# Encoder layer on one core: ssm_b loads moved into SyncE's queue, and another order of the last group's residual, norm and stores

## The chip, the cores and the metric

One Trainium2 chip, one core of it. The metric is the device time of one execution in microseconds; the kernel before took 2082.99 us, the median of three runs (2081.72 to 2086.61). The core has five engines that run their own instruction streams and meet by semaphores: TensorE (PE), VectorE (DVE), ScalarE (ACT), GpSimd (POOL) and SyncE (SP), which here only issues DMAs. GpSimd issues DMAs too, on a software queue of its own.

## The reference

A single encoder layer on 512 tokens of width 1024, all in float32:

```python
h = h + mixer_block(rms_norm(h, g_mix), ...)            # S5 state space + latent attention
h = h + memory_cross_attention(rms_norm(h, g_mem_q), rms_norm(mem, g_mem_kv), ...)
h = h + peer_ffn(rms_norm(h, g_peer), ...)
return rms_norm(h, g_final)

def rms_norm(x, g):
    return x * rsqrt(mean(x * x, -1) + 1e-6) * g
```

The state-space part takes its input matrices from `ssm_b_re` and `ssm_b_im` (2 directions x 32 groups x 64 states x 16 channels each), scaled by a factor made of the decay. `peer_ffn` finds, for each token and each of 8 heads, the best 16 of 16384 experts, gathers a row of `peer_u` and one of `peer_v` for each, and adds up 16 rows of `peer_v`, weighted by a gate times gelu of the dot product of the token with the row of `peer_u`.

## The kernel before, in words

Tokens lie on partitions in 4 tiles of 128. The kernel is written engine by engine, each block in program order; all order between engines comes from semaphores.

**Head.** SyncE issues the constants, the small state-space parameters, the four tiles of x (L582), the norm gains (L588), then weight slabs: `load_slab(n)` (L595) fills one of 3 slots of 1 MB. The first two are the two halves of the input projection ("u"), the third the first latents ("c"). Behind them come copies of `peer_u` and `peer_v` side by side into one table `uv_rows` in HBM (`copy_rows`, L590), which go on between the later slabs. GpSimd issues the four ssm_c loads (L2055) and the four ssm_b loads (L2059), all counted on the semaphore `d_ssm`, then clears some tiles.

ScalarE sums the squares of each x tile as it lands (`squares`, L683), takes the root once VectorE has added epsilon, then an exponential and a sine for the decay (L729 to L731). GpSimd waits for these (L2069) and builds powers of the decay and tables (L2070 to L2127), first small ones, then up to 128 x 1024. PE transposes the normalised x, transposes ssm_c (it waits for all eight loads, L1694), and multiplies by the u slabs. VectorE needs ssm_b from L1198 on. ScalarE takes the first output matrices of GpSimd in `windows` (L754). PE then goes on with lag products, which SyncE spreads with 8 loads per quarter (L618).

**Tail.** `peer_ffn` runs as 32 groups: g = 4 h + t, for head h and token tile t. For each of the 16 experts (slots) of a group GpSimd gathers 128 rows of 8 KB (`row`, L2130) into a ring of 12; it waits until PE has finished the slot that held the place. VectorE makes the dot product (`dot_products`, L1530), ScalarE gelu, gate and a diagonal matrix of the weights (`weigh`, L994), two slots at a time, PE multiplies the diagonal with the row's second half and adds up in PSUM (`slots`, L1951): banks 0 and 1 for even tiles, 2 and 3 for odd ones. VectorE adds the sum to the residual H after a group (`take_sum`, L1539), in the course of the next one.

In the last head each tile also gets its final norm: `final_variance` (square sum over 1024 and epsilon, VectorE, L1547), `final_root` (ScalarE, L990), `final_rows` (reciprocal and scaling by it and by g_final, VectorE, L1552), store (SyncE, L656). For tiles 0 to 2 this lies among the dots of the last group, with all three roots taken together ahead of slots 10 and 11; each is stored as soon as it is scaled. For tile 3 it comes after the last sum. ScalarE swaps its function table (ACT_TABLE_LOAD) when it goes from gelu to the root and back.

Of the kernel before, what the change touches and what calls it, by code (L numbers as in the profile page):

```python
# [232 lines left out]
def encoder_layer(nc, x, mem, positions, g_mix, w_in, b_gate, ssm_lam_re, ssm_lam_im, ssm_log_dt,  # L233
# [4 lines left out]
    with ctx:  # L238
# [3 lines left out]
        def sem(name):  # L242
            return ctx.enter_context(nc.semaphore(name))
# [25 lines left out]
        def reg(lo, *shape, base=R, parts=P):  # L269
# [93 lines left out]
        act_row = reg(27792, TOPK)  # L363
        gel = reg(27808, TOPK)
        junk = reg(17408, D)
        junk1, junk2 = reg(24064, D), held[:, :]
# [9 lines left out]

        d_cst, d_vec, d_par, d_ssm = [sem(n) for n in ("d_cst", "d_vec", "d_par", "d_ssm")]
        d_x = [sem(f"d_x{t}") for t in range(NT)]
# [30 lines left out]
            sem(n) for n in ("dots", "gate_ready", "diag_done", "v_summed")]  # L409
        acc_taken, final_done = sem("acc_taken"), sem("final_done")  # L410
        xg_done = sem("xg_done")

# [161 lines left out]
        def _(sp):  # L574
# [30 lines left out]

            for n in range(SLOTS):
                load_slab(n)
            copy_rows("first")
            for n in range(SLOTS, 5):
# [41 lines left out]
            for h in range(1, PH):  # L651
                sp.wait_ge(q_filled, h * 2)
                sp.dma_start(qw, rows(w_peer_q, h * 256, h * 256 + 256)).then_inc(qw_in, 16)
            for t in range(NT):
                sp.wait_ge(final_done, t + 1)
                sp.dma_start(out[0, P * t:P * t + P, :], xn[:, t, :]).then_inc(d_out, 16)  # L656
            sp.wait_ge(d_out, 16 * NT)

# [7 lines left out]
        def sumsq(k, t):  # L666
            return stat[:, 16 * k + t:16 * k + t + 1]
# [3 lines left out]
        def _(act):  # L671
# [49 lines left out]
            for d in range(2):  # L721
                settle(act.activation(parrow[2][:, 64 * d:64 * d + 64],
                                      dtrow[:, d:d + 1].to_broadcast([G, 64]), ACT.Copy))
            act.activation(parrow[3].rearrange("g (j c) -> g j c", j=CH),
                           drow[:, 0:CG].unsqueeze(1).to_broadcast([G, CH, CG]), ACT.Copy).then_inc(par_rows, 1)
            squares(0, xn, FT[:, 0:2, :].rearrange("p k t -> p (k t)"))

# [282 lines left out]
            def head(h, first=False, last=False):  # L1010
                for t in range(1 if first else 0, NT):
                    g = h * NT + t
                    for b in range(TOPK // 2):
# [6 lines left out]
                        if b == 7 and (not last or t < 2):  # L1020
                            gate_exponentials(g + 2)
                        if last and t == NT - 1 and b == 5:
                            for early in range(NT - 1):
                                final_root(early)
                        if last and t == NT - 1 and b == 7:
                            weigh(g, b, (14,))
                            weigh(g, b, (15,))
                        else:
                            weigh(g, b, (2 * b, 2 * b + 1))
# [25 lines left out]
            head(PH - 1, last=True)  # L1055
            settle(act.activation(gel[:, 0:1], stat[:, 68:69], ACT.Sqrt))
            final_root(NT - 1)


        @block.vector  # L1060
        def _(dve):
# [135 lines left out]
            tt(sm[:, 85, :], sm[:, 85, :], sm[:, 81, :], ALU.mult)  # L1197
            dve.wait_ge(d_ssm, 16 * 8)  # L1198
            fr, fi = (sm[:, 84 + r, :].unsqueeze(2).to_broadcast([P, G, CG]) for r in range(2))
# [358 lines left out]
            def head(h, first=False, last=False):  # L1558

                for t in range(1 if first else 0, NT):  # L1560
# [17 lines left out]
                    if ahead and (not first or t != 2):  # L1578
                        sub_keys((t + 2) % NT)
                    dot_products(g, t, range(5, 8))  # L1580
                    take_sum(g + (-1), (t - 1) % NT)
# [6 lines left out]
                    if last and t == NT - 1:  # L1588
                        final_variance(2)
                        dot_products(g, t, range(10, 11))  # L1590
                        dve.wait_ge(d_frow, 16)
                        for early in range(NT - 1):
                            dot_products(g, t, range(11 + early, 12 + early))
                            final_rows(early)
                        dot_products(g, t, range(14, TOPK))
                    elif last and t == 2:
# [50 lines left out]
            head(PH - 1, last=True)  # L1647
            take_sum(NG - 1, NT - 1)
            final_variance(NT - 1)
            final_rows(NT - 1)  # L1650


        @block.tensor
        def _(pe):
# [38 lines left out]

            pe.wait_ge(d_ssm, 16 * 8)  # L1694
            for r in range(2):
# [253 lines left out]
            early_turns(0)  # L1949
            mem_out(1, 1)  # L1950
            def slots(g, t, some):  # L1951

                for s in some:
                    i = g * TOPK + s
                    pe.wait_ge(diag_done, g * TOPK + (s + 1))
                    v = rings[i % RING]
                    for n in range(2):
                        last = pe.matmul(ps[2 * (t % 2) + n][:, :], diag[s], v[:, D + 512 * n:D + 512 * n + 512],  # L1958
                                         start=(s == 0), stop=(s == TOPK - 1))
                    last.then_inc(v_summed, 1)  # L1960
# [46 lines left out]
            def head(h, first=False, last=False):  # L2007
                for t in range(1 if first else 0, NT):
                    g = h * NT + t
                    ahead = t < 2 and not last  # L2010
                    if not first or t >= 2:
                        pe.wait_ge(acc_taken, g - 1)
                    for n in range(TOPK):
                        slots(g, t, range(n, n + 1))
# [25 lines left out]
        def _(pool):  # L2040
# [12 lines left out]
            for r, w in enumerate((ssm_c_re, ssm_c_im)):  # L2053
                for d in range(2):
                    pool.dma_start(Craw[r][:, :, 64 * d:64 * d + 64],  # L2055
                                 w[0, d].rearrange("(b g) c p -> (g c) b p", b=NB)).then_inc(d_ssm, 16)
            for r, w in enumerate((ssm_b_re, ssm_b_im)):
                for d in range(2):
                    pool.dma_start(bb[r][64 * d:64 * d + 64, :, :],  # L2059
                                 w[0, d].rearrange("g p c -> p g c")).then_inc(d_ssm, 16)  # L2060

# [112 lines left out]
```

## Time and profile before

| | us |
|---|---|
| median of 3 runs (lowest, highest) | 2082.99 (2081.72, 2086.61) |
| profiled execution, as timed | 2079.8 |
| its span in the profile | 2077.5 |
| PE busy | 1784.5 (86%) |
| VectorE busy | 1421.3 (68%) |
| ScalarE busy | 734.3 (35%) |
| GpSimd busy | 709.5 (34%) |

The span runs from the first to the last record of the profiled execution; the time of that execution is 2.3 us longer. Shares of busy time are averages over very different stages. The start and the end of the kernel are short and serial, so there the order in time is to be read, and the waits, not the shares. "DMA share" is the mean busy share of the 16 DMA engines; one engine alone is about 6 to 7%.

### The profile page before, as it was taken

Reading aid. Unit: us, or ns where it says so; the run is one execution under the profiler, and the core shown is the slowest. Engines: PE = TensorE matmul, PEld = TensorE weight load, DVE = VectorE, ACT = ScalarE, POOL = GpSimd, SP = SyncE. Lnnn points to the kernel's source line nnn. Section 1 sums busy time; section 2 is a strip of 40 time slices with the busy share of each in tenths; the row PEclk is TensorE's granted clock in tenths of the full one; section 3 lists DMA queues with packets and bytes.
Section 4 is the critical chain, followed back from the end, with each engine's and each line's share of the span. In section 5 each row is a group of like instructions: output and inputs, shape, how many; then the busy total and the mean of one; then the engine's idle time right before and its main releaser. Section 6 shows DMA issues by size and latency. Waiting matters only on the chain.

```text
span 2077.5 us, 19311 instructions
## 1 busy us (share of the span) xinstructions
PE 1784.5 (86%) x5959; PEld 994.7 (48%) x5959; DVE 1421.3 (68%) x2951; ACT 734.3 (35%) x1949; POOL 709.5 (34%) x659
## 2 busy tenths in 40 slices
PE   5998899999999999899789879888969878987876
PEld 5656434787997675334334334333423333433332
DVE  5894775434453277887777787787677777777765
ACT  3344443222333234343243333333333433343333
POOL 6990000000000034354444444344444444444441
PEclk9998899999999999999989989989999999999999
DMA  9775999888999989999999999999999999999996
GB/s 263 206 197 128 249 294 274 263 249 263 306 282 327 305 323 388 417 421 421 417 421 421 417 421 421 418 421 421 417 418 421 415 408 414 414 418 418 421 414 263
DMA packets 199313, 737.24 MB, mean 355 GB/s; under 512 B 31222, under 2 KB 97963, under 8 KB 133675
## 3 DMA queue, kind: packets, MB, share of 16 engines
q0 software_dynamic: 74112, 537.95, 62.7%
q1 hardware_dynamic: 125098, 198.07, 32.1%
q8 instruction: 47, 0.77, 0.2%
q14 instruction: 56, 0.45, 0.1%
HBM read 731.78 MB, written 136.31 MB: 418 GB/s over the span
## 4 chain that ended last, share of the span: by engine, by line
PE 44%; DMA 25%; DVE 16%; issue 7%; POOL 4%; ACT 4%; SPq 0%; DVEq 0%; ACTq 0%; POOLq 0%
PE bank L1671 23%; PE bank L1958 17%; DMA R<-uv_rows,R 10%; DMA WS<-uv_rows,R 8%; DMA slabs<-uv_rows,R 6%; PE bank L1992 3%; DVE R L1535 2%; PE bank L1660 1%; POOL WS L2049 1%; POOL R L2049 1%; DVE R L1485 1%; DVE R L1488 1%; DVE R L1486 1%; DVE R L1516 1%; DVE R L1519 1%
## 5 line engine op out<-in xcount | busy, mean ns | idle before, releaser
L1958 PE MATMUL bank<-R 128*128 128x512 f32 x1368 | 675.7, 639 | 149.1 <-ACT R L1008 149.0
L2134 POOL DMA_INDIRECT R<-uv_rows,R x342 | 384.8, 1125 | 511.2 <-PE bank L1958 486.7
L1535 DVE CUSTOM_DVE_ANT_0 R<-R,XN 128x1024 f32<-128x1024 f32 x342 | 419.5, 1227 | 169.6 <-DMA R<-uv_rows,R 155.9
L1958 PEld LDWEIGHTS bank<-R 128*128 128x128 f32 x1368 | 272.5, 204 | 525.3 <-issue 311.5
L1001 ACT ACTIVATE R<-R 128x2 f32<-128x2 f32 (+1 forms) x257 | 52.1, 203 | 803.5 <-DVE R L1535 803.1
L2134 POOL DMA_INDIRECT WS<-uv_rows,R x86 | 95.6, 1112 | 687.4 <-DVEq L1522 587.0
L1671 PE MATMUL bank<-R 128*64 128x64 f32 (+6 forms) x776 | 186.0, 387 | 20.0 <-DVE R L1232 7.4
L1958 PE MATMUL bank<-slabs,R 128*128 128x512 f32 x336 | 164.2, 630 | 29.0 <-ACT R L1008 29.0
L1958 PE MATMUL bank<-WS,R 128*128 128x512 f32 x344 | 164.1, 617 | 25.8 <-ACT R L1008 25.8
L1008 ACT ACTIVATE R<-cst,R 128x128 f32<-128x128 f32 x512 | 177.7, 394 | 8.4
L1535 DVE CUSTOM_DVE_ANT_0 R<-WS,XN 128x1024 f32<-128x1024 f32 x86 | 105.4, 1226 | 45.2 <-DMA WS<-uv_rows,R 41.6
L2134 POOL DMA_INDIRECT slabs<-uv_rows,R x84 | 96.8, 1152 | 110.1 <-PE bank L1958 102.5
L1671 PEld LDWEIGHTS bank<-R 128*64 128x64 f32 (+3 forms) x776 | 93.4, 160 | 84.5 <-issue 58.6
L1535 DVE CUSTOM_DVE_ANT_0 R<-slabs,XN 128x1024 f32<-128x1024 f32 x84 | 102.9, 1225 | 42.6 <-DMA slabs<-uv_rows,R 39.5
L1104 DVE TENSOR_TENSOR WSr<-slabs,WSr 128x1024 fp32r<-128x1024 f32 (+2 forms) x46 | 58.4, 1270 | 101.0 <-ACT WSr L709 101.0
L1003 ACT ACTIVATE R<-R 128x1 f32<-128x1 f32 x512 | 123.1, 287 | 8.5
L1992 PE MATMUL bank<-FT,slabs 128*128 128x512 f32 (+1 forms) x256 | 123.2, 574 | 2.4 <-ACT FT L681 2.4
L1958 PEld LDWEIGHTS bank<-slabs,R 128*128 128x128 f32 x336 | 67.0, 202 | 119.4 <-issue 81.3
L1958 PEld LDWEIGHTS bank<-WS,R 128*128 128x128 f32 x344 | 66.8, 197 | 114.3 <-issue 78.5
L1671 PE MATMUL bank<-Rr,WSr 128*128 128x512 f32 (+1 forms) x448 | 95.4, 366 | 0.0
L1671 PEld LDWEIGHTS bank<-Rr,WSr 128*128 128x128 f32 x448 | 77.7, 189 | 13.7
L1071 DVE TENSOR_TENSOR R<-R 128x512 f32<-128x512 f32 (+4 forms) x75 | 65.0, 867 | 18.2 <-PE bank L1671 10.7
(228 smaller groups left out, 2157.3 us busy)
## 6 DMA issues: line engine op xcount, KB each, us to landing
uv_rows<-in_peer_u SPq DMA_DIRECT2D x8, 4096.0 KB, 23.6
uv_rows<-in_peer_v SPq DMA_DIRECT2D x8, 4096.0 KB, 35.3
uv_rows<-in_peer_v SPq DMA_DIRECT2D x10, 2048.0 KB, 13.3
uv_rows<-in_peer_u SPq DMA_DIRECT2D x9, 2048.0 KB, 14.0
uv_rows<-in_peer_u SPq DMA_DIRECT2D x11, 1024.0 KB, 8.2
slabs<-in_w_in SPq DMA_DIRECT2D x17, 512.0 KB, 5.3
slabs<-in_w_mem_kv SPq DMA_DIRECT2D x8, 1024.0 KB, 11.8
slabs<-in_w_peer_q SPq DMA_DIRECT2D x8, 1024.0 KB, 25.4
```

Of the source, the lines that this page charges most:

```text
L1001: settle(act.activation(gel[:, new], act_row[:, new], ACT.Gelu_apprx_tanh))
L1003: ins = act.activation(wgt[:, s:s + 1], gel[:, s:s + 1], ACT.Copy, scale=gate[g % NT][:, s:s + 1])
L1008: act.activation(diag[s], ident, ACT.Copy, scale=wgt[:, s:s + 1]).then_inc(diag_done, 1)
L1071: step(dve.tensor_tensor(out, a, b, op))
L1104: dve.tensor_tensor(lo, src, hi, ALU.subtract).then_inc(w_lo, 1)
L1485: lstep(dve.max_index(ix[:, 0:8], v[:, 0:8], vals))
L1535: dve.tensor_tensor_reduce(prod, rings[i % RING][:, 0:D], xn[:, t, :], 1.0, 0.0, ALU.mult, ALU.add, act_row[:, s:s + 1]).then_inc(dots, 1)
L1671: last = pe.matmul(dst, lhs, rhs, start=(n == 0), stop=(n == len(terms) - 1))
L1958: last = pe.matmul(ps[2 * (t % 2) + n][:, :], diag[s], v[:, D + 512 * n:D + 512 * n + 512], start=(s == 0), stop=(s == TOPK - 1))
L1992: ins = pe.matmul(ps[4 + s][:, cols], qw[:, k, columns(s)], FT[:, k, cols], start=(k == 0), stop=(k == KD - 1))
L2049: step(pool.tensor_tensor(out, a, b, op))
L2134: pool.indirect_dma_start(out=rings[i % RING], out_offset=None, in_=UV, in_offset=bass.IndirectOffsetOnAxis(ap=idx[t][:, s:s + 1], axis=0) ...
```

## The change

Head: the four ssm_b loads leave GpSimd's queue and are issued by SyncE after the first two slabs, ahead of the third; they get a semaphore of their own, `d_ssb`. ScalarE takes a root of a small tile ahead of the squares of x.

Tail, last group (g = 31, tile 3): PE first puts the residual into the banks with an identity matrix, then adds the slots; the sum is not added to H. The square sum of the last tile is made from PSUM, one half by ScalarE and one by VectorE, and the scaling reads PSUM in two halves of 512 columns, each with a store of its own. Stores of tiles 0 to 2 wait until the last dot product is done. The roots are taken ahead of slot 4 (tiles 0 and 1) and ahead of slot 12 (tile 2); slots 12 and 13 are weighed singly too. Scaling of tile 0 comes ahead of dot 7, that of tiles 1 and 2 after dot 15.

```diff
@@ semaphores and a tile of 128 x 1 are added: d_ssb, half_done, half_sq @@
@@ SyncE @@
-            for n in range(SLOTS):
+            for n in range(2):
                 load_slab(n)
+            for r, w in enumerate((ssm_b_re, ssm_b_im)):
+                for d in range(2):
+                    sp.dma_start(bb[r][64 * d:64 * d + 64, :, :],
+                                 w[0, d].rearrange("g p c -> p g c")).then_inc(d_ssb, 16)
+            load_slab(2)
             copy_rows("first")
...
-            for t in range(NT):
+            sp.wait_ge(dots, NG * TOPK)
+            for t in range(NT - 1):
                 sp.wait_ge(final_done, t + 1)
                 sp.dma_start(out[0, P * t:P * t + P, :], xn[:, t, :]).then_inc(d_out, 16)
-            sp.wait_ge(d_out, 16 * NT)
+            for n in range(2):
+                sp.wait_ge(final_done, NT + n)
+                sp.dma_start(out[0, P * (NT - 1):T, 512 * n:512 * n + 512],
+                             xn[:, NT - 1, 512 * n:512 * n + 512]).then_inc(d_out, 16)
+            sp.wait_ge(d_out, 16 * (NT + 1))
@@ ScalarE @@
+            settle(act.activation(stat[0:G, 100:102], dtrow, ACT.Sqrt))
             squares(0, xn, FT[:, 0:2, :].rearrange("p k t -> p (k t)"))
...
-                        if last and t == NT - 1 and b == 5:
-                            for early in range(NT - 1):
-                                final_root(early)
-                        if last and t == NT - 1 and b == 7:
-                            weigh(g, b, (14,))
-                            weigh(g, b, (15,))
+                        if last and t == NT - 1 and b == 2:
+                            final_root(0)
+                            final_root(1)
+                        if last and t == NT - 1 and b == 6:
+                            final_root(2)
+                        if last and t == NT - 1 and b >= 6:
+                            weigh(g, b, (2 * b,))
+                            weigh(g, b, (2 * b + 1,))
...
             settle(act.activation(gel[:, 0:1], stat[:, 68:69], ACT.Sqrt))
+            act.wait_ge(v_summed, NG * TOPK)
+            act.activation(held[:, 0:512], ps[2][:, :], ACT.Square, accum_out=half_sq).then_inc(half_done, 1)
             final_root(NT - 1)
@@ VectorE @@
-            dve.wait_ge(d_ssm, 16 * 8)
+            dve.wait_ge(d_ssb, 16 * 4)
...
-                    dot_products(g, t, range(5, 8))
+                    dot_products(g, t, range(5, 7))
+                    if last and t == NT - 1:
+                        dve.wait_ge(d_frow, 16)
+                        final_rows(0)
+                    dot_products(g, t, range(7, 8))
...
                         final_variance(2)
-                        dot_products(g, t, range(10, 11))
-                        dve.wait_ge(d_frow, 16)
-                        for early in range(NT - 1):
-                            dot_products(g, t, range(11 + early, 12 + early))
-                            final_rows(early)
-                        dot_products(g, t, range(14, TOPK))
+                        dot_products(g, t, range(10, TOPK))
+                        final_rows(1)
+                        final_rows(2)
...
-            take_sum(NG - 1, NT - 1)
-            final_variance(NT - 1)
-            final_rows(NT - 1)
+            dve.wait_ge(v_summed, NG * TOPK)
+            t = NT - 1
+            step(dve.tensor_copy(prod[:, 0:512], ps[3][:, :]))
+            step(dve.tensor_tensor_reduce(prod[:, 512:D], ps[3][:, :], prod[:, 0:512], 1.0, 0.0, ALU.mult, ALU.add, sumsq(4, t)))
+            step(dve.tensor_scalar(sumsq(4, t), sumsq(4, t), 1.0 / D, EPS, ALU.mult, ALU.add))
+            dve.wait_ge(half_done, 1)
+            dve.scalar_tensor_tensor(stat[:, 68 + t:69 + t], half_sq, 1.0 / D, sumsq(4, t),
+                                     ALU.mult, ALU.add).then_inc(var_done, 1)
+            dve.wait_ge(std_done, len(PARTS) + NT)
+            c = stat[:, 76 + t:77 + t]
+            step(dve.reciprocal(c, stat[:, 72 + t:73 + t]))
+            for n in range(2):
+                cols = slice(512 * n, 512 * n + 512)
+                dve.scalar_tensor_tensor(xn[:, t, cols], ps[2 + n][:, :], c, gfrow[:, cols],
+                                         ALU.mult, ALU.mult).then_inc(final_done, 1)
@@ TensorE @@
-            pe.wait_ge(d_ssm, 16 * 8)
+            pe.wait_ge(d_ssm, 16 * 4)
...
+            def residual(t):
+                for n in range(2):
+                    pe.matmul(ps[2 * (t % 2) + n][:, :], ident, H[:, t, 512 * n:512 * n + 512], start=True, stop=False)
...
-                                         start=(s == 0), stop=(s == TOPK - 1))
+                                         start=(s == 0 and g < NG - 1), stop=(s == TOPK - 1))
...
                         pe.wait_ge(acc_taken, g - 1)
+                    if g == NG - 1:
+                        residual(t)
@@ GpSimd @@
-            for r, w in enumerate((ssm_b_re, ssm_b_im)):
-                for d in range(2):
-                    pool.dma_start(bb[r][64 * d:64 * d + 64, :, :],
-                                 w[0, d].rearrange("g p c -> p g c")).then_inc(d_ssm, 16)
```

## Rows read from the trace of the kernel before

**Rows 1.** The page's part 4: the chain that ended last, by engine.

```profile
PE 44%; DMA 25%; DVE 16%; issue 7%; POOL 4%; ACT 4%; SPq 0%; DVEq 0%; ACTq 0%; POOLq 0%
```

**Rows 2.** The chain in order of time, 0 to 200: start, us, what.

```profile
4.47 14.91 DMA XN<-in_x
...
20.72 1.28 ACT L696
...
25.51 0.22 POOL R L2071
...
99.95 0.31 ACT R L762
```

**Rows 3.** Waits, 0 to 110: who waited for whom, us in total, times, longest.

```profile
ACT R L762 <- POOLq L2120: 15.3, 1, 15.3
```

**Rows 4.** Timeline, 0 to 75: start, us, instruction, [idle before, releaser].

```profile
8.95 1.06 ACT L692 ACTIVATE FT<-XN 128x1024 f32<-128x1024 f32 x1 [0.91 <-DMA XN<-in_x]
...
19.47 1.06 ACT L692 ACTIVATE FT<-XN 128x1024 f32<-128x1024 f32 x1 [4.75 <-DMA XN<-in_x]
...
20.79 0.17 DVE L1110 TENSOR_SCALAR stat<-stat 128x4 f32<-128x4 f32 x1 [6.82 <-ACTq L693]
...
31.68 29.94 PEld L1671 LDWEIGHTS bank<-slabs,FT 128*128 128x128 f32 x128
...
48.14 11.16 DVE L1071 TENSOR_TENSOR R<-R 128x32 f32<-128x32 f32 x14
```

**Rows 5.** DMA queues, 5 to 6: packets, MB, share of 16 engines.

```profile
q1 hardware_dynamic: 87, 0.36, 91.6%
```

**Rows 6.** DMA queues, 10 to 15.

```profile
q1 hardware_dynamic: 115, 0.41, 60.3%
q0 software_dynamic: 99, 0.27, 45.3%
```

**Rows 7.** DMA queues, 2054 to 2056.

```profile
q0 software_dynamic: 8, 0.06, 6.9%
```

**Rows 8.** DMA queues, 2060 to 2062.

```profile
q0 software_dynamic: 5, 0.03, 3.9%
```

**Rows 9.** DMA queues, 2064 to 2066.

```profile
q0 software_dynamic: 2, 0.01, 1.0%
```

**Rows 10.** Timeline, 2020 to 2080: the last group.

```profile
2041.37 3.70 PE L1958 MATMUL bank<-slabs,R 128*128 128x512 f32 x8 [1.27 <-ACT R L1008]
...
2051.57 1.28 ACT L992 ACT_TABLE_LOAD   x1
...
2053.27 1.28 ACT L1001 ACT_TABLE_LOAD   x1
...
2053.80 1.23 DVE L1535 CUSTOM_DVE_ANT_0 R<-R,XN 128x1024 f32<-128x1024 f32 x1 [1.13 <-DMA R<-uv_rows,R]
...
2055.82 0.69 ACT L1008 ACTIVATE R<-cst,R 128x128 f32<-128x128 f32 x2
...
2061.59 5.42 PE L1958 MATMUL bank<-R 128*128 128x512 f32 x12 [1.62 <-ACT R L1008]
...
2065.22 1.23 DVE L1535 CUSTOM_DVE_ANT_0 R<-R,XN 128x1024 f32<-128x1024 f32 x1 [2.20 <-DMA R<-uv_rows,R]
...
2067.50 1.98 PE L1958 MATMUL bank<-R 128*128 128x512 f32 x4 [0.49 <-ACT R L1008]
...
2069.59 1.42 DVE L1544 TENSOR_TENSOR H<-bank,H 128x512 f32<-128x512 f32 x2 [3.14 <-PE bank L1958]
...
2073.15 1.28 DVE L1556 SCALAR_TENSOR_TENSOR XN<-H,stat,R 128x1024 f32<-128x1024 f32 x1
```

**Rows 11.** DMA packets, 71 to 72, in the c2 slab's short runs.

```profile
DMA packets 509, 0.06 MB, mean 62 GB/s; under 512 B 509, under 2 KB 509, under 8 KB 509
```

**Rows 12.** Windows: stretch, us; PE, PEld, DVE, ACT, POOL busy; PEclk, DMA, GB/s.

```profile
98.00:114.00 16.00, 12.77 (x61) 6.58 (x60) 15.32 (x15) 9.23 (x16) 15.04 (x12) 0.89 0.00 0
200.00:205.00 5.00, 5.00 (x25) 5.00 (x25) 0.00 (x0) 0.00 (x0) 0.00 (x0) 0.50 0.00 0
```

More of the change, by code:

```diff
@@ L364, in encoder_layer @@
         gel = reg(27808, TOPK)
+        half_sq = reg(27824, 1)
         junk = reg(17408, D)
@@ L375, in encoder_layer @@
         uv_in = [sem(f"uv_in{n}") for n in range(2)]
-        d_cst, d_vec, d_par, d_ssm = [sem(n) for n in ("d_cst", "d_vec", "d_par", "d_ssm")]
+        d_cst, d_vec, d_par, d_ssm, d_ssb = [sem(n) for n in ("d_cst", "d_vec", "d_par", "d_ssm", "d_ssb")]
         d_x = [sem(f"d_x{t}") for t in range(NT)]
@@ L410, in encoder_layer @@
         acc_taken, final_done = sem("acc_taken"), sem("final_done")
+        half_done = sem("half_done")
         xg_done = sem("xg_done")
```

## The prediction

> **What bounds the kernel now.** I read the page's shares of the chain first [rows 1]: PE holds 44% and DMA 25% of it, so no single engine bounds the kernel, and each edit has to be priced in its own stage. The change touches two: the first 30 us and the last 30 us.
>
> In the head, the chain in order of time [rows 2] stands on the load of x from 4.47 us for 14.91 us. Then come the squares of the last x tile, a table load at 20.72, and GpSimd's decay tables from 25.51, which it works off until ScalarE picks up their result at 99.95. ScalarE had waited 15.3 us for that [rows 3]; PE, VectorE and ScalarE have that much room there. So the head is: last x tile, ScalarE, GpSimd, and a microsecond taken from the last tile is taken from all of it.
>
> Why is x late? Its second tile is squared at 8.95 and its fourth at 19.47 [rows 4]: two tiles in 10.5 us. From 5 to 6 us the hardware queue alone moved 0.36 MB in 1 us [rows 5]. From 10 to 15 us it moved 0.41 MB in 5 us, while the software queue, which then carries mostly the ssm_b loads (64-byte runs), held the engines for 45% of the time and moved 0.27 MB [rows 6]. Two x tiles are 1.05 MB.
>
> In the tail, the last group's 16 dot products are paced by gathered rows. From 2054 to 2056 us the software queue fills 6.9% of 16 engines [rows 7]: one engine alone still works off its share of the gathers. When the stores of tiles 0 to 2 come up, its share falls to 3.9% [rows 8] and then 1.0% [rows 9]. Slot 11's dot starts at 2053.80, slot 15's at 2065.22 [rows 10]. Then everything is serial: dot, ScalarE, PE, residual add, square sum, root, scaling, store.
>
> **The change, part by part.** All times are against the profiled execution: span 2077.5 us, 2079.8 us as timed. The median of the three runs, 2082.99, stands 3.2 above it; I take the difference in the profile off the median.
>
> *ssm_b behind the slabs, x tile.* The two tiles after 8.95 would arrive at 0.36 MB/us: 1.05/0.36 = 2.9 us, so tile four at 11.9; I take 12.0, since ssm_c still shares the engines. Bounds: 11.1, where ssm_b's part before 8.95 also goes to x; and 14, where the last megabyte runs at about 0.2. Gain at the last square: 19.47 - 12.0 = 7.5 (5.5 to 8.4).
>
> *Sqrt on dtrow ahead of the squares.* It pulls the 1.28 us table load of 20.72 to about 5.8, where ScalarE waits for x. VectorE's variance step ends at 20.79 + 0.17 = 20.96, so the root could start at 21.0 and not at 22.0: 1.0 us gained. Cover: ScalarE's first square starts about 0.5 us later, which the waits for tiles two to four hide. In the kernel before, Square ran without a load of its own ahead of Sqrt, and I take it to be in both tables; if not, another 1.3 us comes back.
>
> *GpSimd issues four DMAs less.* Its memsets start 4.4 us earlier; they end before the chain needs it, nothing gained. VectorE's small steps that ran beside them may stall at other places, but they feed the exponential only after the roots.
>
> *What is late next.* PE's first product of a slab starts at 31.68 [rows 4], after the change at 23.2. Both u slabs are 2.1 MB: 12.0 + 2.1/0.36 = 17.8, landed by 19 or 20. Then ssm_b: 4 DMAs of 64 x 32 runs are 8192 packets of 64 bytes on the hardware queue. Short packets of the c2 slab ran there at 509 per us at the slowest [rows 11], so 16 us at most; at 1100 it would be 7.5, and I take 8. VectorE needs ssm_b inside the 14 operations that begin at 48.14 [rows 4], after the change near 40; it has landed by 17.8 + 16 + 2 = 36 at worst. Nothing waits.
>
> *Queue behind it.* The third slab and all copies start at 17.8 + X + 2.9 = 20.7 + X, X being the time of ssm_b; in the kernel before they started after 19.4 + 3.15/0.36 = 28.1. From 98 to 114 us the DMA engines stand at 0.00 [rows 12], until the lag loads need them. These come 8.5 earlier, so 7.5 us of the idle 16 are left, and X up to 28.1 - 20.7 + 7.5 = 15 costs nothing. With X = 8 the queue drains before the lag loads, the stages behind see the same order of work as before, and the head's 8.5 us goes through: the copies are released by progress of the compute, so they shift with it. The skill's rule that speaks against the move is in DMA: Bandwidth & Descriptors (Issuing engines are not separate DMA queues): all queues run on the same 16 engines, so another issuer by itself only saves issue time. By it the move from GpSimd to SyncE is worth nothing and all of the gain comes from the order behind x; the sum above uses only the order.
>
> *Stores held back.* The lone engine undisturbed is the 6.9%. The six windows of 2 us from 2054 to 2066 read 6.9, 5.9, 6.9, 3.9, 3.9 and 1.0 (the first, fourth and last stand in [rows 7 to 9]), in all 28.5. At 6.9 throughout, that is 28.5/6.9 x 2 = 8.3 us of work from 2054, so slot 15 lands at 2062.4 and not 2065.1. Slots 12 to 15 then come every 2.15 us after 2053.8, and the dot of slot 15 ends at 2063.7 instead of 2065.22 + 1.23 = 2066.45: 2.75 us.
>
> *Roots split in two, single weighing.* final_root(2) now comes before slot 12: after slots 10 and 11 are weighed (2055.82 + 0.69 = 2056.5) ScalarE loads the root's table, takes the root, loads back: 2 x 1.28 + 0.2 + gaps, free at 2059.4. Slot 12 reaches PE at 2060.4. PE takes 5.42 for three slots [rows 10], with a fourth behind them 5.42 + 1.72 = 7.14: it ends at 2067.6, and is then later than the data (slot 15 alone: 2063.7 + 1.05 + 1.98 = 2066.7). Before: 2067.50 + 1.98 = 2069.5. So of the 2.75 us, 1.9 are kept. Here rule and row part. The row: load 2051.57, three roots, load 2053.27, so a switch costs 1.28 and no more. ScalarE: Activation LUTs (What ACT_TABLE_LOAD costs) gives 1283 ns plus a drain of 1380 for each switch. By the row the sum is as above; by the page two switches end 2.8 us later, a rival below.
>
> *Residual by PE.* Four matmul instructions, 1.72 us, ahead of the last group. PE idles 1.27 us ahead of a pair of slots there, so 0.5 us of delay, caught up by the next pair; gathers are queued 20 us deep. Nothing. If the cover were gone: 0.5.
>
> *End on halves.* Before, from VectorE's 2069.59: two adds (1.42), square sum 1.23 (the operation of the dots) and read-out, variance, root, reciprocal, then 1.28 of scaling from 2073.15, ending 2074.43: 4.84 us. After: copy 0.71 (half of 1.42), half square sum 1.23/2 + 0.1 = 0.72, two small steps 0.4, root and reciprocal as before (0.53), two scalings of a 512 half from PSUM at about 0.72 (the adds read the same halves of PSUM at 0.71): with gaps 3.9. ScalarE's half (about 0.9) lies beside VectorE's 1.4. Gain 0.9. Bounds: 0.4, if reads of PSUM and gaps cost more; 1.2.
> Rows 1 and 2 move behind the last dot: 2 x (0.2 + 1.28) = 3.0 from 2063.7 to 2066.7, inside the wait for PE; were PE on time, they would cost up to 0.1.
>
> *Last store.* Before, from the end of the scaling to the span's end: 2077.5 - 2074.4 = 3.1. Now half of it is already moving and 0.26 MB less is left: 0.5 to 0.9 less, I take 0.7. The three held stores are issued from 2063.7 to 2067 on idle engines and are through before 2071.
>
> Sum: 7.5 + 1.0 + 1.9 + 0.9 + 0.7 = 12.0. 2079.8 becomes 2067.8, the median 2082.99 - 12.0 = **2071.0 us**.
>
> **Rivals.**
> 1. *PE or ScalarE takes the tail* (mechanism of the tables above with a costly switch, or PE's queue longer): slot 12 starts 2.8 us later, PE ends at 2070.4, the tail gives 1.6 - 0.9 = 0.7 instead of 3.5: 2073.8. For it: PE is already the late one in my sum. Against: the rows show a switch at 1.28.
> 2. *Part of the head is lost on the way.* From 200 to 205 us PE is fully busy at a granted clock of 0.50 [rows 12]; where such stretches lie depends on what PE did before. 6 to 8 us more at half speed cost 3 to 4: 2074.5. For it: the clock moved between 0.5 and 1 here; against: the sequence of work is the same, only earlier.
> 3. *ssm_b is not x's brake* (HBM, ssm_c or the descriptors of the slabs are): the head gives 1.0 plus perhaps 1: 2083.0 - 2 - 3.5 = 2077.5. Against: the fall from 0.36 MB/us as the software queue turns to ssm_b.
> 4. *Slower:* 8192 short packets block SyncE's queue. Before, 64-byte runs were 32 to a packet. At X = 30 (273 packets per us, half the slowest row) slab three and the copies are late by 30 - 15 = 15 us at the lag loads, against 12 gained: 2086. It decides from X = 27. Against: 509 per us at the slowest.
> 5. *The change doesn't do what it says*: x is not freed (as in 3), and in the tail the lone engine is slow by itself, so that only the halves remain (0.9 + 0.7, and 1.0 from the table): 2080, within what can't be told from nothing.
>
> **How the numbers follow.** Forecast 0.62; rival 1 0.13; rival 2 0.10; rival 3 0.08; rival 4 0.04; rival 5 0.03. The forecast's own range is 2068 to 2073.5 from its bounds. With rivals 1, 2 and most of 3, and 2 us for the spread of medians (the three runs span 4.9), the range is 2066.5 to 2077.5. A difference under 0.2%, 4.2 us, can't be told from none: faster 0.62 + 0.13 + 0.10 + two thirds of 0.08 = 0.90, same 0.06, slower 0.04.
>
> **What would show it.** Right: the last square starts near 12, GpSimd's wait for the sine ends near 17, ScalarE's window copies start near 91.5; DMA is idle ahead of the lag loads; slot 15's dot starts 11.5 us ahead of the new end (2065.5 - 2054.0), where it was 12.3; PE runs its last four slots without a gap; the tail from the last matmul to the end is 6.4 instead of 8.0. Wrong: a last square after 14, a wait of PE for a u slab or of VectorE for ssm_b that passes the 15.3 us of room, no idle stretch ahead of the lag loads, or a gather share that stays at one engine until late without any store beside it.

## The result and the profile after

The changed kernel takes 2071.01 us, the median of 4 runs (2068.85 to 2073.96); the kernel before takes 2084.13, the median of 4 (2081.72 to 2086.61). The ratio is 0.9944, with a 95% interval of 0.9928 to 0.9961: 11.7 us less, give or take 3.5. The forecast was 2071.0.

The profiled executions differ by less: 2073.96 against 2079.8, spans 2071.4 and 2077.5. The first is the highest of its four runs, and the second lies below all four of its kernel, so the profile shows the mechanism, and has to be asked where 6.1 us of span became 11.7 us of median.

The chain of the changed kernel, shares of the span by engine; it answers to [rows 1]:

```profile
PE 42%; DMA 25%; DVE 16%; issue 8%; POOL 4%; ACT 4%; SPq 0%; DVEq 0%; ACTq 0%; POOLq 0%
```

The same chain in order of time (start, us, what), to be laid beside [rows 2]:

```profile
4.47 8.02 DMA XN<-in_x
...
12.57 1.16 ACT FT L704 x2
...
14.10 0.20 ACT stat L708
...
17.60 0.22 POOL R L2104
```

x is there after 8.02 us of waiting instead of 14.91, no table load stands between the variance and the root, and GpSimd starts at 17.60 instead of 25.51: 7.9 us. The timeline around it (start, us, engine, line, operation, tiles, idle before and what ended it), beside [rows 3, 4]:

```profile
5.67 1.28 ACT L738 ACT_TABLE_LOAD   x1
...
7.20 1.06 ACT L704 ACTIVATE FT<-XN 128x1024 f32<-128x1024 f32 x1
...
12.57 1.06 ACT L704 ACTIVATE FT<-XN 128x1024 f32<-128x1024 f32 x1 [0.21 <-DMA XN<-in_x]
...
24.28 7.97 PE L1701 MATMUL bank<-slabs,FT 128*128 128x256 f32 x33
...
91.59 0.31 ACT L775 ACTIVATE R<-R 128x128 f32<-128x128 f32 x1 [14.01 <-POOLq L2153]
```

The root's table comes in at 5.67, while ScalarE waits for x, and the squares do not ask for another. The first slab product starts 7.4 us earlier and ScalarE's first window copies 8.4 us earlier, at 91.59. ssm_b is on the hardware queue from 17.2 to 23.5. One microsecond of it, 22 to 23:

```profile
DMA packets 1770, 0.11 MB, mean 113 GB/s; under 512 B 1770, under 2 KB 1770, under 8 KB 1770
```

8192 packets in some 6 us. The DMA engines still fall idle ahead of the lag loads: the share of 0.13 below all lies before 97 us, and no packet moves from 97 to 106. The windows (stretch, us; PE, PEld, DVE, ACT, POOL busy; granted clock of PE; DMA share; GB/s) show what happens 40 us later. Changed kernel:

```profile
92.00:106.00 14.00, 12.04 (x61) 6.01 (x61) 13.35 (x14) 9.01 (x15) 13.29 (x10) 0.88 0.13 53
...
142.00:147.00 5.00, 3.05 (x15) 3.06 (x15) 4.83 (x6) 4.67 (x9) 4.65 (x4) 0.50 0.95 205
147.00:152.00 5.00, 5.00 (x25) 5.00 (x25) 2.40 (x4) 0.00 (x0) 0.00 (x0) 0.50 1.00 305
152.00:157.00 5.00, 5.00 (x25) 5.00 (x25) 2.35 (x4) 1.20 (x2) 0.00 (x0) 0.50 0.88 332
157.00:162.00 5.00, 5.00 (x23) 2.39 (x22) 1.74 (x3) 1.91 (x4) 0.00 (x0) 0.79 0.03 14
```

Kernel before, the same piece of work:

```profile
150.00:155.00 5.00, 3.59 (x22) 3.59 (x22) 4.83 (x6) 4.86 (x10) 4.69 (x5) 0.75 0.91 292
155.00:160.00 5.00, 5.00 (x25) 5.00 (x25) 2.82 (x5) 0.00 (x0) 0.35 (x1) 0.50 1.01 306
160.00:165.00 5.00, 5.00 (x29) 4.09 (x29) 3.58 (x6) 2.23 (x4) 0.00 (x0) 0.73 0.55 222
```

A granted clock of 0.50 is PE at 1.2 GHz, 1.00 at 2.4. In the records of the granted clock the changed kernel stands at half speed for 17.1 us here, from 142.0, and the one before for 10.2, from 152.5. The first 2 us of the 17.1 cost nothing, since PE still waits for the lag loads then; what is left is 15.1 against 10.2, and 4.9/2 = 2.4 us. PE's first matmul behind that wait, and the idle time ahead of it, changed kernel and then the one before:

```profile
143.95 0.69 PE L1701 MATMUL bank<-R 128*128 128x64 f32 x2 [4.04 <-DMA R<-XN]
```

```profile
151.41 0.43 PE L1671 MATMUL bank<-R 128*128 128x64 f32 x2 [3.31 <-DMA R<-XN]
```

At these two lines the changed kernel is 7.5 us ahead. The next wait that both have, for ScalarE, ends at the start of these lines of the chain (start, us, what), changed kernel and then the one before:

```profile
169.99 16.52 PE bank L1701 x90
```

```profile
175.15 16.52 PE bank L1671 x90
```

There it is 5.2 us ahead: 26.0 us against 23.7 for the same work, 2.3 us lost, as the clock has it. Another 1.3 are lost up to the first dot product, so in this pair the head's 7.9 us are down to 3.9 there (748.15 before), changed kernel:

```profile
744.29 1.23 DVE L1552 CUSTOM_DVE_ANT_0 R<-WS,XN 128x1024 f32<-128x1024 f32 x1 [1.96 <-DMA WS<-uv_rows,R]
```

The tail, changed kernel, beside [rows 10]:

```profile
2051.07 1.22 DVE L1552 CUSTOM_DVE_ANT_0 R<-R,XN 128x1024 f32<-128x1024 f32 x1 [1.10 <-DMA R<-uv_rows,R]
...
2053.80 1.28 ACT L1005 ACT_TABLE_LOAD   x1
...
2055.31 1.28 ACT L1014 ACT_TABLE_LOAD   x1
...
2057.62 5.42 PE L1993 MATMUL bank<-R 128*128 128x512 f32 x12 [0.38 <-ACT R L1021]
...
2060.96 1.23 DVE L1552 CUSTOM_DVE_ANT_0 R<-R,XN 128x1024 f32<-128x1024 f32 x1 [1.23 <-DMA R<-uv_rows,R]
...
2063.25 1.98 PE L1993 MATMUL bank<-R 128*128 128x512 f32 x4 [0.21 <-ACT R L1021]
...
2065.27 0.69 DVE L1668 COPY R<-bank 128x512 f32<-128x512 f32 x1 [0.16 <-PE bank L1993]
2065.33 0.60 ACT L1073 ACTIVATE held<-bank 128x512 f32<-128x512 f32 x1 [0.62 <-PE bank L1993]
...
2067.54 1.41 DVE L1679 SCALAR_TENSOR_TENSOR XN<-bank,stat,R 128x512 f32<-128x512 f32 x2
2068.32 0.99 SPq L667 DMA_DIRECT2D out<-XN  x2
```

Slots 11 to 15 are 9.89 us apart (before 11.42), each dot waits for its own gathered row, and from slot 11 to the end it takes 20.3 us (before 23.7). The software queue from 2058 to 2060, in the place where the stores had pressed it down in the kernel before [rows 8]:

```profile
q0 software_dynamic: 6, 0.05, 5.8%
```

### The profile page after: what moved, and what is told of

The parts are those of the page before. It is cut to its first block, busy times and chain, and to the rows that moved or that the text cites. A ratio compares the mean times of both kernels' runs of the same rounds, so it can differ in the third digit from the quotient of the medians.

```text
span 2071.4 us, 19329 instructions
## 1 busy us (share of the span) xinstructions
PE 1790.6 (86%) x5963; PEld 995.8 (48%) x5963; DVE 1421.5 (69%) x2952; ACT 737.8 (36%) x1955; POOL 709.0 (34%) x655
## 4 chain that ended last, share of the span: by engine, by line
PE 42%; DMA 25%; DVE 16%; issue 8%; POOL 4%; ACT 4%; SPq 0%; DVEq 0%; ACTq 0%; POOLq 0%
PE bank L1701 23%; PE bank L1993 16%; DMA R<-uv_rows,R 11%; DMA WS<-uv_rows,R 8%; DMA slabs<-uv_rows,R 6%; PE bank L2027 3%; DVE R L1552 2%; POOL R L2086 1%; PE bank L1690 1%; POOL WS L2086 1%; DVE R L1502 1%; DVE R L1505 1%; DVE R L1503 1%; DVE R L1533 1%; DVE R L1536 1%
## 5 line engine op out<-in xcount | busy, mean ns | idle before, releaser
L1701 PE MATMUL bank<-R 128*64 128x64 f32 (+6 forms) x776 | 190.6, 394 | 23.8 <-DVE R L1249 7.4
L1993 PE MATMUL bank<-slabs,R 128*128 128x512 f32 x336 | 163.4, 627 | 25.5 <-ACT R L1021 25.5
L2167 POOL DMA_INDIRECT slabs<-uv_rows,R x84 | 98.1, 1168 | 100.2 <-PE bank L1993 91.5
L1701 PEld LDWEIGHTS bank<-Rr,WSr 128*128 128x128 f32 x448 | 77.7, 189 | 13.7
## 6 DMA issues: line engine op xcount, KB each, us to landing
slabs<-in_w_mem_kv SPq DMA_DIRECT2D x8, 1024.0 KB, 11.3
```

The source lines that it names most:

```text
L1701: last = pe.matmul(dst, lhs, rhs, start=(n == 0), stop=(n == len(terms) - 1))
L2167: pool.indirect_dma_start(out=rings[i % RING], out_offset=None, in_=UV, in_offset=bass.IndirectOffsetOnAxis(ap=idx[t][:, s:s + 1], axis=0) ...
```

## The experiments

Twelve kernels in three batches, each batch on one chip with its own runs of the kernel before: e1 to e4 (25 runs, median 2082.61), e5 to e8 (15, 2082.34) and e9 to e12 (14, 2080.20). Medians are compared within a batch, and over batches by their ratios. Of every profile three times are read: GpSimd's start on the decay tables (head), the first dot product (what is left of the head after 740 us), and slot 11's dot to the end (tail). A fourth is the time that PE's granted clock stood at 0.50 before 740 us, added up over its stretches.

| | median, us | ratio to before (95%) | GpSimd start | first dot | half clock | slot 11 to end |
|---|---|---|---|---|---|---|
| before, profile | | | 25.5 | 748.2 | 54.6 | 23.7 |
| changed, profile | | | 17.6 | 744.3 | 61.4 | 20.35 |
| e1_full | 2070.49 | 0.9945 (0.9923, 0.9966) | 17.4 | 741.2 | 51.2 | 20.35 |
| e2_head | 2073.63 | 0.9961 (0.9946, 0.9977) | 17.7 | 741.4 | 54.6 | 23.7 |
| e3_tail | 2078.40 | 0.9985 (0.9969, 1.0001) | 26.1 | 750.6 | 54.6 | 20.35 |
| e4_move | 2074.66 | 0.9960 (0.9945, 0.9975) | 18.5 | 738.2 | 47.8 | 23.7 |
| e5_hold | 2081.02 | 0.9997 (0.9981, 1.0012) | 25.4 | 745.3 | 47.8 | 22.9 |
| e6_no_hold | 2073.28 | 0.9961 (0.9943, 0.9979) | 18.3 | 743.4 | 58.0 | 20.85 |
| e7_warm2 | 2060.98 | 0.9900 (0.9874, 0.9925) | 17.1 | 732.4 | 30.7 | 20.4 |
| e8_pool_gated | 2069.62 | 0.9934 (0.9911, 0.9956) | 17.5 | 741.2 | 51.2 | 20.3 |
| e9_warm3 | 2057.26 | 0.9893 (0.9877, 0.9910) | 17.6 | 727.2 | 20.5 | 20.35 |
| e10_before_warm3 | 2072.13 | 0.9963 (0.9949, 0.9977) | 25.5 | 739.1 | 23.9 | 23.7 |
| e11_tail_order | 2079.87 | 0.9992 (0.9977, 1.0006) | 25.6 | 750.5 | 58.0 | 22.1 |
| e12_warm_first | 2063.92 | 0.9918 (0.9902, 0.9935) | 17.2 | 735.7 | 44.4 | 20.4 |

**e1_full**: the changed kernel again.

> The whole change once more, as the measure for the others of this call. Theory (sum of parts): head 7.9 us by the profile, of which half-speed stretches of PE at other places take back up to 5, tail 3.4 from the dot of slot 11 on; between 6 and 11.3 us off, by which stretches this execution has. Rival (the gain depends on the length of the gather stage by chance, not on the clock): the PE clock falls in the same stretches as in the kernel before and the time still differs from run to run by 3 us or more.

By its ratio 11.5 us below the kernel before, just over the 11.3 of the expectation, and half-speed time back at 51.2 us. So the long stretch at 142 us is not a fixed price of the change.

**e2_head**: the ssm_b move and the early Sqrt, the tail as before.

> Head alone (ssm_b behind two slabs in SyncE's queue, Sqrt on dtrow); the tail is that of the kernel before. Theory: GpSimd's chain starts at 17.6 instead of 25.5 us (-7.9), slot 11's dot to the end stays 23.7 us, total 3 to 8 us off. The half-speed stretch around 142 to 159 us lasts 17 us as in the whole change, which takes 3.4 back; then the first dot of the gather stage is about 4 us earlier. Rival (the tail changes move the middle): the first dot is 7 or more us earlier here.

**e3_tail**: all edits of the tail, the head as before.

> Tail alone. Theory: GpSimd's chain starts at 25.5 as before, the first dot is where it was within 0.5 us, and slot 11's dot to the end is 20.3 us instead of 23.7: 3.4 us off. Rival (half of it came from an earlier head): less than 2 us in that stretch.

The head alone gives 0.39%, the tail alone 0.15%, both together 0.55%: they add up. Two expectations on the way failed: in e2 the half-speed stretch lasted 10.2 us and not 17, and the first dot came 6.8 us earlier and not 4; in e3, where nothing of the head is changed, it came 2.4 us later and not within 0.5. So a first dot of a single profile is uncertain by more than 2 us, and the "7 or more" of e2's rival was set too near to it. In the profiles the head gives 7.8 at GpSimd's start and the tail 3.3 from slot 11 on. The tail's own median has 1.0 inside its interval: 3.3 us are shown by the trace, not by the timing.

**e4_move**: e2_head without this line:

```diff
-            settle(act.activation(stat[0:G, 100:102], dtrow, ACT.Sqrt))
```

> Only ssm_b is moved; no Sqrt ahead of the squares. Theory: the last x tile is squared at 12.6 as in the whole change, a table load of 1.28 us stands again between the squares and the root, GpSimd's chain starts at 17.6 + 1.0 = 18.6. Rival (Sqrt costs what it saves by holding up the squares): 17.6 or less. And the half-speed stretch near 145 us tells whether 1 us of shift alone moves it.

The chain of waits in order of time:

```profile
12.42 1.16 ACT FT L697 x2
...
13.67 1.28 ACT L701
...
18.46 0.22 POOL R L2072
```

The table load is back between the last square and the root, and GpSimd starts 6.04 us after the last square, against 5.03 in the changed kernel (17.60 - 12.57): 1.0 us for the preload. The medians of e2 and e4 (2073.63, 2074.66) can't show it; the trace does.

**e5_hold**: the kernel before with the held stores only.

```diff
+            sp.wait_ge(dots, NG * TOPK)
             for t in range(NT):
```

> The kernel before with one edit: SyncE waits for the last dot product before it stores anything. Theory (the stores of tiles 0 to 2 share the lone DMA engine with the last gathers): slot 15's dot starts 1.4 to 1.6 us sooner after slot 11's (9.9 instead of 11.4), and the time from slot 11's dot to the end falls by as much; the last store may wait for the three held ones and give some of it back, up to 1 us. Rival (the lone engine is slow by itself; the 1.5 us came from VectorE and ScalarE being free of the final rows and roots): slot 11 to slot 15 stays above 11 us.

Slot 15's dot came 9.86 us after slot 11's, and still only 0.8 us is left at the end. PE, VectorE's add, and its scaling:

```profile
2057.45 7.13 PE L1959 MATMUL bank<-R 128*128 128x512 f32 x16 [1.62 <-ACT R L1009]
```

```profile
2064.70 1.42 DVE L1545 TENSOR_TENSOR H<-bank,H 128x512 f32<-128x512 f32 x2 [3.94 <-PE bank L1959]
```

```profile
2068.25 1.29 DVE L1557 SCALAR_TENSOR_TENSOR XN<-H,stat,R 128x1024 f32<-128x1024 f32 x1
```

With the old order PE is the late one: 16 matmul instructions in one piece, VectorE waiting 3.94 us for them. From the start of slot 15's dot to the add it takes 5.17 us, where it was 4.37 [rows 10], and that is the whole 0.8 given back. Against the expectation, the last store gives back nothing: from the end of the scaling (2069.54) to the end of the span it takes 3.1 us as before, though three held stores went ahead of it. Holding the stores alone isn't worth anything that a timing shows.

**e6_no_hold**: the changed kernel without that wait.

> The whole change without the hold: tile 0 is stored while the last slots are gathered (its scaling comes ahead of dot 7); tiles 1 and 2 are scaled after the last dot in any case. Theory: one store of three falls on the gathers, so slot 11 to slot 15 grows from 9.9 by about a third of 1.5 us, 0.5, or by nothing if the store is done before slot 12's turn on the lone engine; total within 0.6 of the whole change. Rival: it grows by 1 us or more.

Slots 11 to 15 take 9.89 us here too: scaling of tiles 1 and 2 stands behind the last dot, so their stores come late by themselves, and tile 0's is through before slot 12. The 0.5 us at the end come from elsewhere. PE, and PE's window from 2052 to 2056:

```profile
2051.20 12.19 PE L1992 MATMUL bank<-R 128*128 128x512 f32 x24 [2.13 <-ACT R L1020]
```

```profile
2052.00:2056.00 4.00, 4.00 (x8) 1.65 (x7) 1.67 (x4) 3.83 (x9) 0.00 (x0) 0.69 0.06 27
```

A half-speed stretch fell into the tail of that execution, and PE's last matmul ends 4.8 us after slot 15's dot starts, against 4.3 in the changed kernel: that is the 0.5. So with the new order the explicit wait adds nothing that was measured (its ratio, 0.9961, and that of the whole change overlap). With the old order the wait alone brings the same 9.9 us (e5). Either edit takes the stores off the last gathers, and that is what counts.

**e8_pool_gated**: ssm_b goes back to GpSimd's queue, but behind the last x tile.

```diff
+            pool.wait_ge(d_x[NT - 1], 16)
+            for r, w in enumerate((ssm_b_re, ssm_b_im)):
+                for d in range(2):
+                    pool.dma_start(bb[r][64 * d:64 * d + 64, :, :], ...).then_inc(d_ssb, 16)
```

> The whole change, but the four ssm_b loads stay on GpSimd's software queue and are issued once the last x tile has landed. It tells the order from the queue. Theory (x is late because ssm_b runs beside it; the queue does not matter): last square at 12.6 as in the whole change, GpSimd's chain starts at 17.6, since the issuing (4.4 us) ends near 17; the u slabs now share the engines with ssm_b and land up to 8 us later, PE's first product of a slab moves from 23.5 to at most 31, inside the 15 us of room. Rival (SyncE's hardware queue is what helps, with 64-byte runs cheaper there): the chain starts later than 19 or the windows of ScalarE come 2 us later than in the whole change.

GpSimd starts at 17.48, the first dot is at 741.2, as in e1_full to 0.1 us. ScalarE's windows start at 92.06 against 91.35 in e1_full, less than the 2 us of the rival, and PE's first product of a slab at 24.42. The queue is of no matter here, the order is: ssm_b beside x is what held x up.

**e7_warm2, e12_warm_first, e9_warm3, e10_before_warm3**: PE transposes an identity matrix into a bank that is free at that moment while it would wait; the results are overwritten and unused. e12 has only the first block, 32 transposes ahead of the product at 144 us, and e7 a second of 56 ahead of the last output product. e9 has three, and e10 the same three (`keep_busy` takes a free bank and makes the given number of transposes; `kvn` is the place ahead of the turns of the gelu result):

```diff
             def block_outputs(q):
+                if q == 1:
+                    b = take(pe, ("Y", q))
+                    for n in range(34):
+                        pe.transpose(b[:, columns(n % 4)], ident, ident)
+                if q == 3:
+                    keep_busy(("D", 3, NB - 1), 66)
...
+            keep_busy(("kvn",), 18)
```

> The whole change, plus 32 transposes of the identity where PE waits for the lag loads of quarter 1 (near 140 us) and 56 where it waits for VectorE ahead of the last output product (near 186 us); their results are not used. Theory (the half-speed stretches near 142 to 159 and 190 to 210 us come of PE standing idle just before, and cost half their length where PE is on the chain): the granted clock stays at 1.00 through both, the first dot of the gather stage comes 8 to 15 us earlier than in the whole change without them. Rival (the clock follows something else, such as total load, or PE isn't on the chain there): the stretches stay, or go and the first dot moves by less than 3 us.

> The whole change with the 32 transposes near 138 us alone. Theory (each stretch costs by itself): half speed from 142 to 159 goes, from 190 to 210 stays, and the third scan quarter of VectorE begins near 163.5 as with both sets, but the first dot is only 6 to 9 us earlier than the 741 to 744 of the whole change, about 735. Rival (the second stretch depends on the first): it goes as well and the first dot comes to 732 or less.

> The whole change with PE kept busy in three waits: 34 transposes of the identity near 138 us, 66 ahead of the last output product (in a bank that is free at once), 18 ahead of the turns of the gelu result; none of their results is used. Theory (PE's idle time before a stretch sets the granted clock): the stretch near 186 to 200, half speed in the kernel with 32 and 56 transposes where a gap of 1.3 us was left, runs at 1.00 as well; the last output product takes 5.8 instead of about 9 us, and the first dot of the gather stage comes 2 to 5 us earlier than the 732.4 there. Rival (the clock falls there whatever PE does): the stretch stays, the first dot within 1.5 us of 732.4.

> The kernel before with the same transposes and nothing else changed. Theory (the two gains are independent, since both go by the same chain): first dot 10 to 16 us earlier than the 748.2 of the kernel before, total 10 to 15 us off; against the whole change with the transposes it stands 11 us behind (7.9 head, 3.4 tail), and that difference shows the head's full gain, which the clock hid in the first comparison. Rival (the gain of the transposes exists only with the earlier head): less than 5 us off.

PE in e7, where a gap of 1.28 us was left at the second place, and the window behind it:

```profile
184.37 0.41 PE L1701 MATMUL bank<-R 128*128 128x64 f32 x2 [1.28 <-DVE R L1249]
```

```profile
137.00:147.00 10.00, 9.86 (x83) 9.10 (x82) 9.69 (x10) 6.71 (x15) 8.96 (x7) 1.00 0.95 251
186.00:200.00 14.00, 11.76 (x59) 10.77 (x58) 6.70 (x6) 3.89 (x19) 0.00 (x0) 0.51 0.43 72
```

And in e9, with the gap filled:

```profile
184.29 0.41 PE L1701 MATMUL bank<-R 128*128 128x64 f32 x2 [0.19 <-DVE R L1249]
```

```profile
147.00:160.00 13.00, 11.79 (x113) 7.92 (x112) 6.10 (x10) 8.16 (x14) 0.00 (x0) 1.00 0.54 156
...
183.00:200.00 17.00, 13.91 (x125) 13.22 (x123) 8.10 (x8) 7.20 (x35) 0.00 (x0) 0.96 0.47 87
```

At each place the half speed goes when PE is kept busy ahead of it, and only there: e12 cures the first and leaves the stretch at 183.5, and e7's second place was cured only when the gap was filled. The time follows the clock: from the first matmul of the product near 144 us to the wait for ScalarE behind it, it takes 18.75 us in e9 (141.64 to 160.39) and in e10 (151.68 to 170.43) alike, 26.0 in the changed kernel and 23.7 in the one before. The first dots of e12, e7 and e9 are at 735.7, 732.4 and 727.2.

On the kernel before, the blocks of e9 give 9.1 us at the first dot and 7.7 us of the median (0.37%, interval 4.8 to 10.6), where 10 to 16 and 10 to 15 were expected: more than the rival's 5, less than forecast. On the changed kernel they give about 11 us by the two ratios (0.9893 against 0.9944). Whether the gain of the transposes is the same on both can't be told from that. e9 and e10 differ by 14.9 us in median and 11.9 at the first dot, where 11 in all were expected, but 10.0 of the 11.9 are there ahead of the first transposes, where e10's execution has a half-speed stretch of 3.4 us near 105 and e9's has none; and e9's profile is of the fastest of its four runs. e9 is the best version run, 1.07% below the kernel before.

**e11_tail_order**: the kernel before with the new order of roots, scalings and single weighing and the held stores, but the old sum, variance, scaling and whole last store.

> The kernel before with the tail's order alone: hold, final rows 1 and 2 behind the last dot, roots in two parts, slots 12 and 13 weighed singly; the last tile still goes through the add to H, one square sum, one scaling and one store. Theory: slot 11 to slot 15 takes 9.9 us, the end follows slot 15's dot by 12.1 less the gain of the singly weighed slots, about 12.1; from slot 11 to the end 22.0 to 22.2, that is 1.5 of the tail's 3.4 us, the other 1.8 being the add by PE and the halves (1.1 on VectorE, 0.65 in the store). Rival (the three held stores delay the last one, as with the hold alone, where 0.8 came back): 22.9.

The scaling of tiles 1 and 2 fills VectorE's wait, and it idles only 0.16 us ahead of the last sum:

```profile
2070.72 1.42 DVE L1549 TENSOR_TENSOR H<-bank,H 128x512 f32<-128x512 f32 x2 [0.16 <-PE bank L1969]
```

From slot 11 to the end it takes 22.1 us: order and hold are worth 1.6 (23.7 to 22.1), residual by PE and halves 1.7 more (22.1 to 20.35).

## Why the prediction was right, step by step

*x tile, 7.5 forecast.* The last square starts at 12.57 and not at 12.0: 6.9. That ssm_b beside x was the brake (against rival 3) is shown by e4, where in the head nothing but its place and issuer changed, and by e8, where its issuer stayed and only its place changed. By the Trainium skill, DMA: Bandwidth & Descriptors (Issuing engines are not separate DMA queues), DMAs of all issuers run on the same 16 engines, and another issuer saves only the time to issue. e8 agrees: GpSimd starts at 17.48, against 17.43 in e1.

*Sqrt ahead of the squares, 1.0.* e4 against the changed kernel: 1.0. Head in all 7.9 against 8.5.

*Time X of ssm_b, 8.* It was 6, with 917 to 1770 packets in a microsecond (in the slowest, 19 to 20, hardly any moved for the first 0.3 us). Rival 4 needed 27 us; it is refuted. Its premise was also misread: in the kernel before ssm_b stood on the software queue as 128 packets of 4 KB, so 64 of the short runs to a packet and not 32. The mark of 91.5 for the window copies was met at 91.59.

*What is late next, nothing.* Of the two rivals to this, only rival 2 is real in single executions: the profiled one lost 2.3 us of the head to a longer half-speed stretch near 150 us, and 1.3 more up to the first dot. Over profiles it comes out nearly even. New head without transposes (changed, e1, e2, e4, e6, e8): 54.0 us of half clock on average, first dot at 741.6; old head (before, e3, e5, e11): 53.8 and 748.7. So 7.0 us of the 7.8 reach the first dot, which so few profiles can't tell from all of it (738.2 to 744.3 with the new head, 745.3 to 750.6 with the old), and my argument that the sequence of work is the same, only earlier, held for the average alone. The spans of the first pair are thereby explained: 3.9 at the first dot, 3.3 in the tail, and 1.1 the other way from the first dot to slot 11, a stage that took from 1304.2 to 1306.8 us in the profiles.

*Held stores, 2.75, of which 1.9 kept.* The mechanism held, but two terms of the sum were mis-sized. The gathers' pace was read as 2.15 us from a share of 6.9%; undisturbed it is 2.47, so slot 15's dot gained 1.5 and not 2.75. The share of one engine in windows of 2 us is a coarse number: in the changed kernel it reads 6.9, 6.9, 5.9, 6.9 and 5.8, on average 6.5. With 6.5 the forecast's working, 28.5/6.5 x 2, puts the end of the gathers 0.5 us later. The packets themselves give the pace: the lone engine takes the eight packets of 8 KB of a gather one by one, a new one every 0.31 us, in both kernels; in the kernel before from 2060.4 on, with the stores of tiles 0 to 2 on the same engine, most come every 0.46, and slots 14 and 15 take it 2.8 and 3.7 us. The second term was left out: a dot starts 0.6 us after the last packet of its gather (2064.61 and 2065.22 before, 2060.38 and 2060.96 after), and the forecast let slot 15's start with it. Together that is 1.1 of the 1.25 us of the miss.

Because the data of slot 15 came later than forecast, PE was not late: its last slot starts 0.21 us after it last worked and waits for ScalarE. So all of the 1.5 was kept, near the 1.9 of the sum. The marks that hung on a late PE failed with it: slot 15's dot starts 10.5 us ahead of the end and not 11.5, and PE's last four slots are two pieces. From the last matmul to the end it takes 6.2 us, forecast 6.4. That the stores held up the gathers is shown twice, by the wait alone (e5, 9.86) and by the new order without the wait (e6, 9.89). The wait as such is not needed beside the order, and without the order it gives half of its gain back to PE.

*Root in two parts.* The two loads at 2053.80 and 2055.31 take 1.28 each, with the root at 2055.09 between: a switch and back cost 2.8 us. The drain in the Trainium skill, ScalarE: Activation LUTs (What ACT_TABLE_LOAD costs), does not appear here, and rival 1 falls.

*Residual by PE, nothing.* Its four matmul instructions took 1.88 us at 2027.31, among gathers that the rest waits for: no delay seen.

*Halves, 0.9, and last store, 0.7.* From VectorE's first step (2065.27) to the end of the scaling (2068.95) 3.7 us against 4.84: 1.1. From there to the end 2.45 against 3.1: 0.6. Sum 1.7, the same as e11 against the changed kernel.

In all: 7.9 + 1.5 + 1.1 + 0.6 = 11.1 us, of which 7.0 + 3.3 = 10.3 reach the end by the averages of the profiles; 12.0 were forecast, and 11.7 (8.1 to 15.0) and 11.5 (7.1 to 16.0) measured. The medians can't tell 10.3 from 12, so the exact hit of the forecast is luck beyond that. Rival 5 is out with the ratio.

## What to carry to other kernels

In a serial head, put first on the queues what the chain waits for, and everything of short runs behind it; which engine issued it did not matter here. At the end, keep table loads, scalings and stores of finished tiles out from between the last operations on which the end hangs, and look at which engine is last before crediting a gain: half of what the wait taken away in e5 gave went to the next engine that was late, PE. When a kernel is moved by microseconds, compare PE's granted clock stage by stage before reading anything into the difference of two spans, and where PE waits a few microseconds ahead of a long product on the critical path, try giving it unused work up to the last moment of the wait; 1.3 us left open undid it here (e7).

## What the runs showed of the hardware

PE's idle time costs more than its length. At gaps of 7.4, 4.0, 3.3 and even 1.3 us ahead of a product its granted clock fell to 1.2 GHz for stretches of 20.5, 17.1, 10.2 and 13.7 us; with the first two places filled by transposes it stayed at 2.4 through the products there, worth about 11 us on the changed kernel by the ratios. In the ten profiles without transposes the gap near 144 or 151 us was 2.5 to 3.4 us where the stretch lasted 10.2, and 3.4 to 4.6 us where it lasted 13.7 or 17.1; this goes together, and no run sets the gap apart from the rest. The half-speed time before 740 us differs between executions of the same kernel (61.4 and 51.2 us in the changed one), and makes up most of what one profile differs from the next in this stage: the first dots of the six profiles with the new head lie 6.1 us apart, and 2.0 when half of the half-speed time is taken off.

The last group's rows are finished by one DMA engine at 2.47 us for each gather of 1 MB, when the other fifteen are done, and stores issued then take turns with them on that engine (0.46 us from packet to packet instead of 0.31). Short runs of 64 bytes passed the hardware queue at 917 to 1770 packets in a microsecond by themselves, yet beside x on the software queue, there 64 of them to a packet of 4 KB, they pressed x down to 0.41 MB in 5 us [rows 6].
